# A two-block transformer kernel: weight parts split by halves of a chunk, and norm factors spread by two products of rounded parts

## What is computed

```python
def second_block(x, mem, ...):                      # DEPTH_2 = 2 layers
    for l in range(DEPTH_2):
        h = rmsnorm_2(x, pre_norm_g[l])             # pre-norm
        z = h @ w_in[l]
        q_lat, kv_lat, k_pe, gb, gc, xin, q_mem, gate = split_cols(z)
        q = rmsnorm_2(q_lat, q_norm_g[l]) @ w_uq[l]         # query norm
        kv = rmsnorm_2(kv_lat, kv_norm_g[l]) @ w_ukv[l]     # key and value norm
        a_out = mla_attention(...)                  # 8 heads
        c_out = short_gated_conv(gb, gc, xin, conv_w[l])
        mem_n = rmsnorm_2(mem, mem_norm_g[l])
        m_out = memory_attention(q_mem, mem_n, w_mk[l], w_mv[l])   # keys: mem_n @ w_mk
        y = concatenate([a_out, c_out, m_out]) * silu(gate)
        x = x + rmsnorm_2(y @ w_o[l], post_norm_g[l])       # post-norm
```

## Time and profile before

| | |
|---|---|
| median of three runs | 2219.17 us |
| profiled execution | 2219.24 us |
| its span | 2217.4 us |
| TensorE busy | 2196.1 us (99%) |
| DVE busy | 1365.2 us (62%) |
| ACT busy | 814.3 us (37%) |
| TensorE on the chain that ended last | 94% |
| DVE and ACT on it | 3% and 2% |
| HBM traffic | 136 GB/s over the span |

### The profile page before, as it was taken

The page is one execution under the profiler, slowest core; times in us unless marked ns, Lnnn a source line. Parts: engine busy times, 40 slices in busy tenths (PEclk is TensorE's granted clock), DMA queues, the critical chain, the costliest instruction groups (busy, mean ns, idle before and its releaser), DMA issues.

```text
span 2217.4 us, 27523 instructions
## 1 busy us (share of the span) xinstructions
PE 2196.1 (99%) x10348; PEld 1823.1 (82%) x10348; DVE 1365.2 (62%) x1952; ACT 814.3 (37%) x1232; POOL 114.9 (5%) x151
## 2 busy tenths in 40 slices
PE   8999999999999999999999999999999999999998
PEld 7888888888888888888888888888888888888887
DVE  6677788874248543567667732385434677677665
ACT  6333434442235421334333532244213443335221
POOL 0100001001110100000000011101000000000000
PEclk9999999999999999999999999999999999999999
DMA  7455544453247222225444432373222153435432
GB/s 279 167 158 153 166 150 152 144 186 112 95 145 265 84 95 99 76 76 158 133 135 124 165 117 95 128 270 113 97 95 74 65 157 125 144 115 157 172 119 108
DMA packets 89852, 303.05 MB, mean 137 GB/s; under 512 B 7408, under 2 KB 48624, under 8 KB 66480
## 3 DMA queue, kind: packets, MB, share of 16 engines
q1 hardware_dynamic: 83760, 271.33, 37.3%
q10 hardware_dynamic: 4608, 16.78, 2.0%
q0 software_dynamic: 1408, 13.89, 1.7%
HBM read 253.74 MB, written 48.23 MB: 136 GB/s over the span
## 4 chain that ended last, share of the span: by engine, by line
PE 94%; DVE 3%; ACT 2%; issue 1%; DMA 0%; ACTq 0%; POOL 0%; DVEq 0%; SPq 0%; POOLq 0%
PE acc L542 71%; PE sc L542 11%; PE ov L542 6%; DVE lo L1355 2%; ACT hi L992 1%; PE ov L701 1%; PE sc L688 1%; PE sc L687 1%; PE sc L882 1%; PE sc L883 1%; PE acc L722 0%; PE acc L723 0%; PE acc L557 0%; PE acc L561 0%; PE acc L558 0%
## 5 line engine op out<-in xcount | busy, mean ns | idle before, releaser
L542 PE MATMUL acc<-h_hi,hi 128*128 128x512 f32 x2240 | 880.0, 393 | 10.6 <-DVE h_lo L1424 8.1
L542 PE MATMUL acc<-h_lo,hi 128*128 128x512 f32 x2240 | 873.2, 390 | 0.0
L542 PE MATMUL acc<-h_hi,lo 128*128 128x512 f32 x2240 | 872.8, 390 | 0.0
L1355 DVE TENSOR_TENSOR lo<-raw,hi 128x2048 fp32r<-128x2048 f32 (+2 forms) x194 | 427.3, 2203 | 390.1 <-ACT hi L992 388.4
L992 ACT ACTIVATE hi<-raw 128x2048 fp32r<-128x2048 f32 (+2 forms) x194 | 358.1, 1846 | 471.9 <-PE acc L542 311.2
L542 PEld LDWEIGHTS acc<-h_hi,hi 128*128 128x128 f32 x2240 | 421.2, 188 | 104.4 <-issue 12.6
L542 PEld LDWEIGHTS acc<-h_hi,lo 128*128 128x128 f32 x2240 | 421.0, 188 | 88.6
L542 PEld LDWEIGHTS acc<-h_lo,hi 128*128 128x128 f32 x2240 | 421.3, 188 | 86.2 <-issue 1.4
L1067 ACT ACTIVATE prob<-prob,st 128x256 f32<-128x256 f32 x128 | 63.6, 498 | 110.5 <-DVE st L1485 110.5
L999 ACT ACTIVATE sq<-acc 128x512 f32<-128x512 f32 x32 | 19.2, 600 | 224.2 <-PE acc L542 217.3
L1305 ACT ACTIVATE prob<-sc,st 128x512 f32<-128x512 f32 x64 | 44.1, 689 | 43.7 <-DVE st L1901 43.7
(11 more groups left out here) (291 smaller groups left out, 2791.9 us busy)
## 6 DMA issues: line engine op xcount, KB each, us to landing
raw<-w_dram SPq DMA_DIRECT2D x170, 1024.0 KB, 4.9
turned<-pt SPq DMA_DIRECT2D x32, 512.0 KB, 3.2
pt<-turned SPq DMA_DIRECT2D x64, 256.0 KB, 4.9
turned<-pt SPq DMA_DIRECT2D x32, 448.0 KB, 3.0
pt<-turned SPq DMA_DIRECT2D x64, 224.0 KB, 4.0
xr<-residual ACTq DMA_DIRECT2D x16, 512.0 KB, 5.3
residual<-g ACTq DMA_DIRECT2D x16, 512.0 KB, 4.6
raw<-w_dram SPq DMA_DIRECT2D x8, 896.0 KB, 5.8
```

Source lines behind the costliest of these rows:

```text
L542: ins = pe.matmul(to, a, b, start=first and n == 0, stop=last and n == 2)
L1355: dve.tensor_tensor(lo[c.slot][:, 0:width], raw[c.slot][:, 0:width], hi[c.slot][:, 0:width].bitcast(F32), ALU.subtract).then_inc(lo_done, 1)
```

## The change

Two things are changed.

1. For the four key chunks of the memory in each layer, and for the first gate chunk of each second head, ACT and DVE make the parts in two halves of 1024 columns each. ACT counts the first half on a new semaphore, `hi_half`, and the second on `hi_done`; DVE waits for each in turn and counts `lo_done` after its second half. TensorE waits for `lo_done`, as before.
2. For the eight norms of the second block, the factors are split into a rounded part `r_hi` and the rest, a diagonal block is made of each, and TensorE multiplies rounded ones by both, adding up. The ones are rounded once, in place, by ACT in the first block. The two spreads of the first block stay as they are.

The core of the diff:

```diff
@@ -57 @@
     QRT, KVRT = 4, 2
+    HALVED = len(KEYS) + MLA // 2
@@ -160 @@
         area = sb("area", 4096)
-        cst = sb("cst", C_COLS)
+        c0 = free[0]
+        cst, ones_r = sb("cst", C_COLS), sb("ones_r", P, F32R, at=c0 + 4 * ONES)
...
         cs = sb("cs", S)
-        zt, posi = sb("zt", S, at=free[0]), sb("posi", S, I32, at=free[0])
+        zt0 = free[0]
+        zt, posi = sb("zt", S, at=zt0), sb("posi", S, I32, at=zt0)
@@ -172 @@
         r_x, qt, r_h = sqacc, dg, g[:, (KT - 1) * S:KT * S]
-        st = sb("st", 104)
+        s0 = free[0]
+        st, r_hi = sb("st", 104), sb("r_hi", TB, F32R)
+        dg_hi, dg_kv_lo, dg_lo = sb("dg_hi", S, F32R, at=s0 - 4 * S), sb("dg_kv_lo", S, F32R, at=m1 + 2048), sb("dg_lo", S, F32R, at=zt0)
@@ -273 @@
-        hi_done, lo_done, chunk_done = sem("hi_done"), sem("lo_done"), sem("chunk_done")
+        hi_done, lo_done, chunk_done, hi_half = sem("hi_done"), sem("lo_done"), sem("chunk_done"), sem("hi_half")
@@ -653 @@
-            def sums(count_on, squares, of=sqacc):
+            def sums(count_on, squares, of=sqacc, one=ones_r[:, 0:1].bitcast(F32)):
...
                 for b in range(TB):
-                    ins = pe.matmul(ov[0][:, b:b + 1], of[:, tile(b, P)], ones[:, 0:1], start=True, stop=True)
+                    ins = pe.matmul(ov[0][:, b:b + 1], of[:, tile(b, P)], one, start=True, stop=True)
@@ -668 @@
+            def spread_parts(no, to, low_=dg_lo):
+                pe.wait_ge(diag_done, no + 1)
+                pe.matmul(to, ones_r[:, :], dg_hi[:, :], start=True, stop=False)
+                pe.matmul(to, ones_r[:, :], low_[:, :], start=False, stop=True).then_inc(r_done, 1)
...
                 pe.wait_ge(consts_in, 16)
-                sums(x_added, ODD + 1)
+                sums(x_added, ODD + 1, one=ones[:, 0:1])
@@ -789 @@
                 sums(added, sq_no(l, PREN) + 2)
-                memory_keys(0, ov[1][:, 0:MEM], 12, lambda: spread(norm_no(l, POSTN), bank(0)))
+                memory_keys(0, ov[1][:, 0:MEM], 12, lambda: spread_parts(norm_no(l, POSTN), bank(0)))
@@ -803 @@
                     pe.wait_ge(mk_in, l * 2 + 2)
-                    spread(norm_no(l, PREN), bank(1))
+                    spread_parts(norm_no(l, PREN), bank(1))
...
                 features(chunk2(l, KVL + 1), h_hi, h_lo)
-                spread(norm_no(l, QN), bank(0))
+                spread_parts(norm_no(l, QN), bank(0))
...
                         features(chunk2(l, CONV + j, i, 6), h_hi, h_lo)
-                spread(norm_no(l, KVN), bank(1))
+                spread_parts(norm_no(l, KVN), bank(1), dg_kv_lo)
@@ -991 @@
+            def split_halves(c):
+                act.wait_ge(loaded[c.slot], (c.uses + 1) * 16)
+                act.wait_ge(chunk_done, c.n + (1 - c.back))
+                for n in range(2):
+                    part = tile(n, CW // 2)
+                    act.activation(hi[c.slot][:, part], raw[c.slot][:, part], ACT.Copy).then_inc((hi_half, hi_done)[n], 1)
@@ -1084 @@
             act.wait_ge(r_done, 2)
+            act.activation(ones_r[:, :], ones, ACT.Copy)
@@ -1152 @@
                 output(l)
-                split(chunk2(l, MEMORY + 1), MW[1])
+                split_halves(chunk2(l, MEMORY + 1))
@@ -1160 @@
                         n = 3 + SPLIT_AT.index(t)
-                        split(chunk2(l, MEMORY + n), MW[n])
+                        if n in KEYS:
+                            split_halves(chunk2(l, MEMORY + n))
+                        else:
+                            split(chunk2(l, MEMORY + n), MW[n])
@@ -1310 @@
                         split(chunk2(l, HEAD + 3 * j + 3, i, 6), HW[1 - j])
-                        split(chunk2(l, HEAD + 3 * j + 4, i, 6))
+                        if j == 0:
+                            split_halves(chunk2(l, HEAD + 4, i, 6))
+                        else:
+                            split(chunk2(l, HEAD + 7, i, 6))
@@ -1355 @@
+            def split_halves(c, count):
+                for n in range(2):
+                    part = tile(n, CW // 2)
+                    if n == 0:
+                        dve.wait_ge(hi_half, count)
+                    else:
+                        dve.wait_ge(hi_done, c.n + 1)
+                    ins = dve.tensor_tensor(lo[c.slot][:, part], raw[c.slot][:, part], hi[c.slot][:, part].bitcast(F32), ALU.subtract)
+                ins.then_inc(lo_done, 1)
@@ -1379 @@
+            def diagonals(link, low_=dg_lo):
+                link.then(dve.tensor_copy(r_hi[:, :], r))
+                link.then(dve.tensor_tensor(nt, r, r_hi[:, :].bitcast(F32), ALU.subtract))
+                for diag, part in ((dg_hi, r_hi[:, :].bitcast(F32)), (low_, nt)):
+                    for b in range(TB):
+                        ins = dve.tensor_scalar(diag[:, tile(b, P)], ident, part[:, b:b + 1], None, ALU.mult)
+                ins.then_inc(diag_done, 1)
...
                 newton(no, link, n)
-                diagonal(n, diag)
+                if no < 2:
+                    diagonal(n, diag)
+                else:
+                    diagonals(link)
@@ -1397 @@
                 link.then(dve.tensor_tensor(r, r, r_rows, ALU.mult))
-                diagonal()
+                diagonals(link, dg_lo if no % 4 == QN % 4 else dg_kv_lo)
...
             def norm_links(l, which):
-                return Links(norm_link, l * 21 + (8, 12, 17, 23, 29)[which - 2])
+                return Links(norm_link, l * 29 + (8, 14, 21, 29)[which - 2])
@@ -1671 @@
                 output(l)
-                split(chunk2(l, MEMORY + 1), MW[1])
+                split_halves(chunk2(l, MEMORY + 1), l * HALVED + 1)
@@ -1698 @@
                         n = 3 + SPLIT_AT.index(t)
-                        split(chunk2(l, MEMORY + n), MW[n])
+                        if n in KEYS:
+                            split_halves(chunk2(l, MEMORY + n), l * HALVED + (KEYS.index(n) + 1))
+                        else:
+                            split(chunk2(l, MEMORY + n), MW[n])
@@ -1932 @@
                     dve.tensor_tensor(dg[:, :], acc[gb.slot][:, :], r_h, ALU.mult).then_inc(evacuated[gb.slot], 1)
-                    if not last:
-                        split(chunk2(l, HEAD + 3 * j + 4, i, 6))
+                    if not last and j == 0:
+                        split_halves(chunk2(l, HEAD + 4, i, 6), l * HALVED + len(KEYS) + 1 + i)
+                    elif not last:
+                        split(chunk2(l, HEAD + 7, i, 6))
```

## The result

The changed kernel takes 2207.18 us, the median of five runs (2207.04 to 2207.78), beside 2218.62 for the kernel before on the same chip (2218.43 to 2219.57): 11.44 us faster, ratio 0.9948, 95% interval 0.9937 to 0.9959. The forecast was 2207.8 and 11.4 less. The profiled execution took 2207.46, its span 2205.7.

What follows compares the result with a forecast made beforehand. TensorE, busy 99% of the span, was taken as the bound. Gates 4.4, keys 3.4 and 1.2, spreads 3.3, less 0.5 post-norm and 0.4 latent chunk: 11.4 us off 2219.24, so 2207.8; range 2205.5 to 2212.9.

Steps and rivals of the forecast that it cites:

- Gates: First gate of each second head, eight times: halving removes the whole stall, 0.55 us each, 4.4 us in all.
- Keys: Memory key chunks: second to fourth of each layer 0.56 us each, 3.4; first of each layer 0.59 each, 1.2.
- T: The time at which ACT starts the high parts of a chunk; 664.60 for the key chunk worked out.
- rival (a): DVE is the bound of the memory stage, so the keys' 3.4 us is not had: 2211.2 us; chance 0.15.
- Spreads: Eight norm spreads: two products of rounded parts take 0.454 us instead of 0.86, saving 0.41 each, 3.3 us.
- Post-norm: The memory's norm: its longer chain makes the spread 0.15 us late, 0.26 with restart, costing 0.5 in both layers.
- Pre-norm: Its chain grows by 1.28 us with 1.65 in hand before the spread, so nothing is lost.
- The value product: Product of the head before, next on TensorE after the gate: brought nearer by no more than 0.55 us.
- Second latent chunk: First layer only: low parts ready at 694.0, TensorE wants them at 693.7; a loss of 0.4 us.

Runs made afterwards that it cites:

- the experiment: The changed kernel with one more dependent DVE copy of four columns in each pre-norm's chain: 2210.20 us, against 2208.37 for the changed kernel on the same chip.
- halves alone: The changed kernel with the eight spreads in float32 as before, the halved chunks kept: 2210.38 us, 8.5 faster than the kernel before, ratio 0.996.

## Why the prediction was right, and where not

**Gates: right.** 0.52 at the one worked out, against 0.55 for the mean one; all eight waits went, and came back together with the whole chunks. The differences of start times across the eight gates add up to 4.6, where 4.4 was forecast.

**Keys: right, with too small a remnant.** The waits for the low parts went in the first trace but for one: the fourth key chunk of layer two was 0.19 late with 0.11 of restart. The forecast had the halves "ready at T + 3.75 to 3.85", just in time, and priced a miss at 0.1. DVE's start (T + 1.42 at the third chunk) was as forecast to 0.05. What I left out was that T moves with TensorE and the load does not: with TensorE earlier, the chunk ahead waits for its DMA, and the whole unbroken list hangs on that. The forecast did see that the low parts of the values chunk before come 0.84 later behind the longer chain, but asked only whether TensorE would wait for them; that the next load starts at their end was left out. The third key chunk of layer one was late by 0.40, 0.51 and 0.77 in the three later traces of the changed kernel. That is a part of the gap between its best median and its worst, and rival (a) in small, with another cause than the one I named: a transfer at the head of DVE's list, and the norm chain ahead of that transfer, not the list's length in a period alone.

**Spreads: right, a little low.** 0.41 each was read from the start of the second product behind; the float32 product also stretches the pitch of those behind it, and the whole is 0.45 to 0.46. The Trainium skill, "FP8 and Floating Point Precision", section "TensorE Precision Notes", counts four passes for a true float32 product; two of four at 0.227 give an estimate of 0.45, and this trace agrees better with that than with my row. Where a row and a rule differ by 0.05, a later anchor would have told which.

**Post-norm: right** to 0.07 a layer. **Pre-norm: right, by luck.** 0.42 in hand was forecast as 0.37, and the chain still met GpSimd's additions twice, as before. But whether GpSimd's addition came 0.1 before or after the last diagonal was beyond what I could read, and the experiment priced it at 1.8 us. The Trainium skill, "SBUF — State Buffer", section "Who interferes with whom", says that the two engines hold a shared pair of ports exclusively; the 1.25 beside 0.16 and the 1.89 beside 0.87 agree. Not every overlap costs, though: in the trace of before fifteen of DVE's reductions (1.22 us, over 128x1024, in the first block) ran beside a GpSimd instruction for some 0.6 us and took no longer than the others.

**The value product: wrong.** "Nothing of it is brought nearer by more than the 0.55": in the first pair it was brought nearer by 0.8. TensorE came 5.02 earlier to the product ahead of it (1008.42 and 1003.40), ACT's start on the transposed weights only 4.20 (1005.67 and 1001.47). And there was less in hand than that: a value product that waits starts 2.46 to 2.47 behind ACT's start, in all 18 late cases of these traces, and before it stood 2.98 behind, so 0.5 was in hand. I had looked at a steady pair, where the product stood 4.95 behind (1076.06 and 1081.01), with 2.5 in hand. The two stalls, 0.73 together, are more than the whole 0.6 by which the gates fell short. Why the transfer comes so late in the first pair was not pursued, nor why the lateness varies: in the traces with halved gates, two-part spreads and the product in its place it is 0.17 to 0.39 in the first layer and 0.07 to 0.28 in the second, with halves alone 0.10 and 0.05.

**Second latent chunk: wrong**, 0.4 that did not come. I held the transfer at its old 8.0 us; it landed in 6.0.

So the agreement is partly cancellation. The profiled executions differ by 11.78, 0.4 more than forecast: 0.65 in the first block, which nothing in the forecast covers, 0.3 for spreads and 0.4 for the latent chunk on one side, 0.3 of keys and 0.6 of gates on the other. The medians differ by 11.44.

## What to carry to other kernels

A pipeline of engines that feeds TensorE through two buffers can be tightened by handing over halves, and each stall of 0.25 to 0.3 that it ends is worth about twice its idle. When TensorE gains, the transfers and the other engines' lists stay where they were: look at every consumer between the edit and the end in its first round, not in its steady one, and write down what each has in hand. Where something lands within 0.1 us of its need, put its consumer a tile later; moving two of them by one tile took both stalls out of the trace, though in times it is 1.3 us between medians whose ranges overlap. And where an engine's list grows, ask also which loads it releases, not only who waits for its results.

## What the hardware did that I had not expected

A stall too short to be listed still costs: a product that started 0.09 late behind 256-column products was followed after 0.33 instead of 0.23. The slower start isn't over with the first product: behind a float32 product of ones with a diagonal the next eight stood 0.23 on average apart, where they are 0.227 apart otherwise, and behind a plain stall of 0.25 the next six did. One load of 768 KB, released at the same point of the program, reached its consumer after 4.9 us in one execution and 5.7 in another, and after 5.5 with half of the residual's traffic left out, where it was nearly all that moved meanwhile.
